# Low parts of the query weights by GpSimd, half of the second stream's choices during the query projection, and three split buffers in the dense expert sum

## The reference, cut to what matters

```
q = (h @ w_q).reshape(b, l, PEER_HEADS, 2, PEER_KEY_DIM // 2)
s = einsum('blhpk,hpnk->blhpn', q, sub_keys)
sv, si = top_k(s, 16)
cand = sv[..., 0, :, None] + sv[..., 1, None, :]
cv, ci = top_k(cand, 16)
expert = i1 * 128 + i2           # i1, i2: keys picked by ci
gate = softmax(cv)
act = gelu(einsum('tkd,td->tk', u[expert], h))
out = einsum('tk,tkd->td', gate * act, v[expert])
x = x + g2 * out; y = rmsnorm(x, final_g)
```

## Time and profile before

| | us |
|---|---|
| median of three timed runs | 3150.67 (3147.31 to 3153.22) |
| the profiled execution | 3154.65 |
| its span, first to last instruction | 3152.6 |
| busy: PE / DVE / ACT / POOL | 2352.2 / 2236.9 / 1229.7 / 1153.3 |
| query projection, from the first half of wq to the last copy of its result | 1713 to 1816 |
| u stretch, to the last `expert_act` | 1816 to 2511 |
| scatter of stream 1 | 2512 to 2592 |
| dense v, 128 iterations | 2593 to 3134 |
| last adds, norm, stores | 3134 to 3153 |

### The profile page before, as it was taken

How to read it: one execution, slowest core, us unless ns; L and a number is a source line. 1 busy time by engine, 2 the same in 40 slices (tenths; PEclk the granted TensorE clock), 3 DMA queues, 4 the chain that set the end, 5 groups by cost and what they waited for, 6 DMA issues and landing times.

```text
span 3152.6 us, 38773 instructions
## 1 busy us (share of the span) xinstructions
PE 2352.2 (75%) x15046; PEld 2063.5 (65%) x15046; DVE 2236.9 (71%) x2892; ACT 1229.7 (39%) x1951; POOL 1153.3 (37%) x773
## 2 busy tenths in 40 slices
PE   6899999999989998999998910000330079998997
PEld 2588889988877887999987910000330068786886
DVE  1344446878888753444545899999999889895885
ACT  1233334555455643433343300001990184342433
POOL 0000000255645510000000032787888647674660
PEclk8899999999999999999999955555555579997999
DMA  9888775545444478766553487999999869996993
GB/s 380 335 308 290 292 294 191 191 142 175 147 154 157 155 258 327 282 243 226 191 187 134 148 335 251 405 422 422 422 421 422 360 187 373 352 364 225 329 370 132
DMA packets 149033, 866.74 MB, mean 275 GB/s; under 512 B 17858, under 2 KB 30162, under 8 KB 70626
## 3 DMA queue, kind: packets, MB, share of 16 engines
q1 hardware_dynamic: 67698, 447.32, 38.7%
q0 software_dynamic: 70992, 406.08, 33.3%
q10 hardware_dynamic: 10160, 10.88, 1.0%
HBM read 836.81 MB, written 27.39 MB: 274 GB/s over the span
## 4 chain that ended last, share of the span: by engine, by line
PE 53%; DVE 14%; POOL 13%; DMA 8%; issue 8%; ACT 3%; DVEq 0%; SPq 0%; ACTq 0%; POOLq 0%
PE bank L1682 30%; POOL u_ring L673 13%; PE bank L2049 8%; PE bank L1668 7%; DMA raw<-in_tiles 3%; PE bank L1707 2%; DVE w_lo L1098 2%; DMA v_got<-in_v_rest,expert 2%; DVE u_ring L1561 2%; DMA u_ring<-in_peer_u,expert 2%; PE bank L2032 2%; DVE conv L1212 1%; DVE peer_g L1589 1%; DMA v_raw<-in_v_dense 1%; DVE y_w L1270 1%
## 5 line engine op out<-in xcount | busy, mean ns | idle before, releaser
L1098 DVE TENSOR_TENSOR w_lo<-raw,w_hi 128x1024 fp32r<-128x1024 f32 x482 | 638.6, 1339 | 573.8 <-ACT w_hi L716 568.9
L716 ACT ACTIVATE w_hi<-raw 128x1024 fp32r<-128x1024 f32 x482 | 501.1, 1058 | 654.0 <-PE bank L1682 347.9
L673 POOL DMA_INDIRECT u_ring<-in_peer_u,expert x256 | 479.9, 1875 | 411.4 <-PE bank L1682 212.9
L1682 PE MATMUL bank<-h_lo,w_hi 128*128 128x256 f32 x2048 | 594.0, 290 | 26.3 <-DVE w_lo L1098 17.3
L1561 DVE CUSTOM_DVE_ANT_0 u_ring<-u_ring,h_t 128x2048 f32<-128x2048 f32 x256 | 580.4, 2289 | 28.4 <-DMA u_ring<-in_peer_u,expert 26.7
L1682 PE MATMUL bank<-h_hi,w_lo 128*128 128x256 f32 x2048 | 583.0, 285 | 0.0
L1682 PE MATMUL bank<-h_hi,w_hi 128*128 128x256 f32 x2048 | 582.8, 285 | 0.0
L1682 PEld LDWEIGHTS bank<-h_lo,w_hi 128*128 128x128 f32 x2048 | 396.2, 193 | 69.2 <-issue 30.5
L680 POOL DMA_INDIRECT v_got<-in_v_rest,expert x256 | 342.5, 1338 | 229.1 <-DVE peer_g L1589 180.8
L1682 PEld LDWEIGHTS bank<-h_hi,w_lo 128*128 128x128 f32 x2048 | 396.7, 194 | 0.9
L1682 PEld LDWEIGHTS bank<-h_hi,w_hi 128*128 128x128 f32 x2048 | 396.1, 193 | 0.0
(11 more groups left out here) (304 smaller groups left out, 4568.9 us busy)
## 6 DMA issues: line engine op xcount, KB each, us to landing
raw<-in_tiles SPq DMA_DIRECT2D x337, 1024.0 KB, 5.4
v_raw<-in_v_dense SPq DMA_DIRECT2D x128, 660.0 KB, 6.9
s_t<-in_states POOLq DMA_DIRECT2D x8, 512.0 KB, 7.0
y_hi_rows<-y_hi_e POOLq DMA_DIRECT2D x16, 256.0 KB, 2.4
y_lo_rows<-y_lo_e POOLq DMA_DIRECT2D x16, 256.0 KB, 6.2
gate_rows<-gate_buf ACTq DMA_DIRECT2D x8, 512.0 KB, 4.6
y_hi<-y_hi_rows POOLq DMA_DIRECT2D x1, 4096.0 KB, 27.4
y_lo<-y_lo_rows POOLq DMA_DIRECT2D x1, 4096.0 KB, 17.0
```

The costliest lines, as they stand in the source:

```text
L673: pool.indirect_dma_start(u_ring[:, U_SLOT[e]], None, a["peer_u"][0], bass.IndirectOffsetOnAxis(ap=expert[:, s, k:k + 1], axis=0)).then_in ...
L716: act.activation(w_hi[:, i % RING], raw[:, slot % SLOTS, (n % 2) * 2 * CH:(n % 2 + 1) * 2 * CH], ACT.Copy) \
L1098: dve.tensor_tensor(w_lo[:, i % RING], raw[:, n // 2 % SLOTS, (n % 2) * 2 * CH:(n % 2 + 1) * 2 * CH], w_hi[:, i % RING].bitcast(F32), ALU. ...
L1682: ins = pe.matmul(spot if x.shape[1] == KT else spot.rearrange("p (s t) -> p s t", s=NS), w[:, col], moving, start=start and k == 0 and m ...
```

## The change

1. The low parts of the 32 halves of wq are made by POOL, with a semaphore of their own (`lo_wq`), in front of its gathers. DVE does none of them.
2. `choose(1, 0)` and `choose(1, 1)` run on DVE during the projection, right behind `choose(0, 0)` and `choose(0, 1)`. With no w_lo to place, DVE goes on in the list at one pause alone, counted over the chooses of a block (pause 9, 5, 1, 0 for j = 0, 1, 2, 3), where it copies the result of the next block (L1525). The semaphores of the choices are kept by stream, and `choose(1, 2)` and `choose(1, 3)` alone have an `expert_act` in their pauses.
3. Dense v has three split buffers instead of two, and three raw buffers instead of four. SP no longer waits for the scatter in front of raw tile 3.
4. The eight spreads of g2 lie behind every second iteration (64, 66, ... 78) instead of every one, and ACT's copies at 68, 70, ... 82. SP's loads of the rows of g2 and final_g move from i = 34 to 42, that of x3 from 98 to 106, with the same waits.

```
-TABLE = 4
+TABLE = 3
+DENSE = 3
@@ SP
-                        sp.wait_ge(lo_done, SPLIT_NO[last] + 1)
+                        if SPLIT_NO[last] < WQ_NO:
+                            sp.wait_ge(lo_done, SPLIT_NO[last] + 1)
+                        else:
+                            sp.wait_ge(lo_wq, SPLIT_NO[last] + 1 - WQ_NO)
...
-                if i == TABLE - 1:
-                    sp.wait_ge(scat_done, NS * BATCHES)
...
-                if i == 34:
+                if i == 42:
                     sp.wait_ge(dense_done, 32)
...
-                if i == 98:
+                if i == 106:
                     sp.wait_ge(dense_done, 96)
@@ POOL
+            for i in range(WQ_NO, len(SPLIT)):
+                n = SPLIT[i]
+                pool.wait_ge(hi_done, i + 1)
+                pool.wait_ge(split_used, SPLIT[i - RING] + 1)
+                pool.tensor_tensor(w_lo[:, i % RING], raw[:, n // 2 % SLOTS, (n % 2) * 2 * CH:(n % 2 + 1) * 2 * CH],
+                                   w_hi[:, i % RING].bitcast(F32), ALU.subtract).then_inc(lo_wq, 1)
@@ ACT
-                if i >= 2:
-                    act.wait_ge(dense_done, i - 1)
-                act.activation(v_hi[:, i % 2], v_raw[i % TABLE][:], ACT.Copy).then_inc(v_hi_done, 1)
+                if i >= DENSE:
+                    act.wait_ge(dense_done, i - DENSE + 1)
+                act.activation(v_hi[i % DENSE][:], v_raw[i % TABLE][:], ACT.Copy).then_inc(v_hi_done, 1)
...
-                if 68 <= i < 76:
-                    n = i - 68
+                if 68 <= i < 84 and i % 2 == 0:
+                    n = (i - 68) // 2
@@ DVE
-                if n not in SPLIT_NO:
+                if n not in SPLIT_NO or SPLIT_NO[n] >= WQ_NO:
                     return
...
+            def pause(j):
+                if pauses[0] == (9, 5, 1, 0)[j]:
+                    advance_to(min(FIRST["wq", j] + 2 * HALVES + LEAD, N_HALVES + LEAD))
+                pauses[0] += 1
 
             for j in range(4):
                 advance_to(min(FIRST["wq", j] + HALVES + LEAD + 3, N_HALVES + LEAD))
-                limit = min(FIRST["wq", j] + 2 * HALVES + LEAD, N_HALVES + LEAD)
-                choose(0, j, lambda: next_half(limit))
+                pauses[0] = 0
+                choose(0, j, lambda: pause(j))
+                if j < 2:
+                    choose(1, j, lambda: pause(j))
...
-            for j in range(4):
+            for j in range(2, 4):
                 choose(1, j, take)
@@ PE
-                if 64 <= i < 72:
-                    n = i - 64
+                if 64 <= i < 80 and i % 2 == 0:
+                    n = (i - 64) // 2
```

More of the change, by code:

```diff
@@ L312, in program @@
         coef_d = at("coef_d", [P, NS, N_KEYS, P], F32, 0)
[L314 to L318, removed]
+        v_raw = [at(f"v_raw{n}", [P, V_DENSE], F32, kib) for n, kib in enumerate((191, 196.15625, 145))]
+        v_hi = [at(f"v_hi{n}", [P, V_DENSE], F32R, kib) for n, kib in enumerate((152, 157.15625, 177))]
+        v_lo = [at(f"v_lo{n}", [P, V_DENSE], F32R, kib) for n, kib in enumerate((128, 133.15625, 171.84375))]
+        c_hi = [at(f"c_hi{n}", [P, NS, P], F32R, kib) for n, kib in enumerate((162.5, 163.5, 182.25))]
+        c_lo = [at(f"c_lo{n}", [P, NS, P], F32R, kib) for n, kib in enumerate((164.5, 165.5, 183.25))]
         v_got = [at(f"v_got{n}", [P, V_REST], F32, kib) for n, kib in
@@ L428, in program @@
         score_in = sem("score_in")
-        gate_max = sem("gate_max")
+        gate_max = [sem(f"gate_max{s}") for s in range(NS)]
         gate_exp = sem("gate_exp")
-        chosen = sem("chosen")
+        chosen = [sem(f"chosen{s}") for s in range(NS)]
         x2_saved = sem("x2_saved")
@@ L487, in _ @@
             sp.dma_start(x2_rows, x2_t[:]).then_inc(x2_saved, 16)
-            sp.wait_ge(chosen, 4 * NS)
+            for s in range(NS):
+                sp.wait_ge(chosen[s], 4)
             sp.wait_ge(split_used, N_HALVES)
@@ L1386, in choose @@
                                               in1=keyf[:, s, 1, mine], op0=ALU.mult, op1=ALU.add))
-                dve.tensor_copy(expert[:, s, mine], key_f[:]).then_inc(chosen, 1)
+                dve.tensor_copy(expert[:, s, mine], key_f[:]).then_inc(chosen[s], 1)
             def normalise(s):
@@ L1593, in dense_lo @@
                 dve.wait_ge(v_hi_done, i + 1)
-                if i >= 2:
-                    dve.wait_ge(dense_done, i - 1)
-                dve.tensor_tensor(v_lo[:, i % 2], v_raw[i % TABLE][:], v_hi[:, i % 2].bitcast(F32), ALU.subtract) \
+                if i >= DENSE:
+                    dve.wait_ge(dense_done, i - DENSE + 1)
+                dve.tensor_tensor(v_lo[i % DENSE][:], v_raw[i % TABLE][:], v_hi[i % DENSE][:].bitcast(F32), ALU.subtract) \
                     .then_inc(v_lo_done, 1)
@@ L1993, in _ @@
                 if n in SPLIT_NO:
-                    pe.wait_ge(lo_done, SPLIT_NO[n] + 1)
+                    if SPLIT_NO[n] < WQ_NO:
+                        pe.wait_ge(lo_done, SPLIT_NO[n] + 1)
+                    else:
+                        pe.wait_ge(lo_wq, SPLIT_NO[n] + 1 - WQ_NO)
                 work(n)
```

24 lines of the change are left out of this document (11 added, 13 removed).

## The result

The changed kernel takes 3112.17 us (median of four runs, 3107.02 to 3116.14) where the kernel before takes 3148.99 on the same chip (four runs): ratio 0.9887, 95% interval 0.9858 to 0.9916, 36.8 us less. A second comparison on another chip, with nine runs of before, gave 3108.27 against 3153.57, ratio 0.9856 [0.984, 0.9873]. The forecast was 3117, in a range from 3094 to 3138.

What follows compares the result with a forecast made beforehand. It took PE and DVE to bound the projection, DVE then DMA the u stretch, DVE dense v, except a stall at g2. Terms -38 - 1.3 + 3 + 2.7 = -33.6 from 3150.7 gave 3117 us, range 3094 to 3138.

Steps and rivals of the forecast that it cites:

- g2 every second iteration: Dense v, iterations 66 to 75: 41 us lost to stalls, 3 of PE's delay reaching DVE; gain 38 us, bounds 34 and 41.
- the 4.35 us: Dense v: the part of PE's 7.4 us delay from eight spreads that the third split buffer absorbs before DVE is held.
- the ring: At g2 in dense v: PE waits for ACT's copy, which ACT cannot reach before PE ends another iteration; 41.0 us lost.
- Start of dense v: v_hi(2) no longer waits for PE's iteration 0, so v_lo(2) starts at about 2597.8 instead of 2599.13: -1.3 us.
- Three raw buffers: Dense v: one raw buffer fewer leaves loads less time to land; cost +3 us, bounds -5 and +12.
- My slack of 8.4 us: Dense v: the time a raw load may take to land with three raw buffers, against 12.1 with four.
- rival C: Dense v: raw buffers starve the loop, 3170 us, marked by ACT's v_hi waiting over 50 us for v_raw; chance 0.05.
- Projection and u stretch: DVE's freed work moves the u stretch's end by -22.3 us, POOL's lock gives back 25: +3 us, bounds -22 and +26.
- c: What POOL's w_lo costs DVE in lock waits during the chooses: 25 us, bounds 0 and 48.
- The price of w_lo on POOL: Query projection: no row had w_lo on POOL; the nearest, L601, takes 2.41 us at least, 2.70 in the median.
- Rival B: Query projection: POOL's w_lo takes 2.7 us or more and short casts are locked too, 3137 us; chance 0.13.
- PE's stops behind the copies: Query projection: PE waits about 8 us at blocks 1 and 2 for DVE's late result copies; nobody waits for PE.

Runs made afterwards that it cites:

- projection part alone: Against the kernel before: only w_lo of wq moved to POOL and choose(1, 0), choose(1, 1) made early, dense v untouched; 3151.69 us, ratio 1.0009.
- spacing alone: Against the kernel before: only g2's spreads and copies moved to every second iteration, with two split and four raw buffers; 3120.19 us, ratio 0.9905.
- buffers alone: Against the kernel before: only dense v's three split and three raw buffers, no scatter wait, g2's spreads still at eight iterations in a row; 3110.82 us, 0.9881.
- two pieces: Against the changed kernel: each w_lo on POOL made by two 128x512 instructions instead of one 128x1024; run twice, 3104.24 and 3104.68 us.
- four pieces with a wait: Against the changed kernel: each w_lo on POOL in four 128x256 instructions, an already met semaphore wait ahead of each; 3123.3 us, ratio 0.9894.
- four-piece runs: Against the changed kernel: each w_lo on POOL in four 128x256 instructions, no added wait; run twice, 3120.65 and 3120.39 us.

## Why the prediction was right, point by point

**g2 every second iteration, -38.** Measured -40.7 between iterations 66 and 75, and PE falls behind as worked out: in the chain of waits after, a pair of iterations is 7.43 us of matmuls and one spread (1.12 in its record, 1.05 in the chain), 8.49 from pair to pair (8.4 predicted).

```profile
2852.78 7.43 PE bank L2067 x36
2861.25 7.43 PE bank L2067 x36
2869.73 7.44 PE bank L2067 x36
```

Part of the lag comes out behind iteration 75: the 37 iterations to 112 are 3.5 us longer. 40.7 - 3.5 is 37.2, beside the 38. How long the stall is varies by itself: with the dense part untouched (projection part alone) iterations 66 to 75 take 68.91 us instead of 74.75, and 75 to 112 take 150.26 instead of 147.18. Taken over 66 to 112, the two executions of the untouched dense part average 220.6 and the nine with both edits 184.3: 36.2 us, still close to the 38. The two ends that I gave are measured too: spacing alone, nothing absorbed, was put at 34 and gives 32 to 35; the 4.35 us for what a third split buffer absorbs is 5.5, from one execution. What the prediction had wrong is the attribution. It gave the 38 us to the spacing, and the run with the buffers alone reaches 35.6 without it (623.1 to 587.5): each of the two edits opens the ring, and the second adds about 5.

**Start of dense v, -1.3.** From L to v_lo of iteration 2 pass 89.1 us instead of 90.1: -1.0.

**Three raw buffers, +3: mis-sized.** The runs with three and four raw buffers give -3, within what executions differ by, and from v_lo of iteration 2 to that of 66 pass 245.5 to 251.4 us in the ten executions with three raw buffers and both of SP's waits moved, 248.8 to 252.0 in the three with four: no cost is seen, and 0 or a little less is what the runs allow. My slack of 8.4 us was not contradicted; the landings of 2595 to 2760 are 6.4 to 11.5 us with a median of 7.3 (before), and only the tail of them passes it. That tail is shorter with three raw buffers: in nine executions 4 to 11 landings of iterations 5 to 109 are over 8.4 us, where there were 18. But the step counted every stop of v_raw as one of DVE. The waits from 2590 to 3090 after the change:

```profile
ACT v_hi L1030 <- DMA v_raw<-in_v_dense: 211.9, 92, 9.6
ACT v_hi L1030 <- PE bank L2067: 71.2, 33, 4.1
DVE v_lo L1611 <- ACT v_hi L1030: 26.9, 19, 2.0
DVE peer_g L1604 <- DMA v_got<-in_v_rest,expert: 19.8, 23, 3.3
```

ACT waits 211.9 us for v_raw. I had written that over 50 would be rival C. As a marker that was wrong: with three split buffers ACT is free to run ahead of PE, so it stands at the load, where it used to stand at PE (291.1 us for PE and 15.8 for v_raw in the same stretch before). The run with three raw and two split buffers shows that it is the split buffer: there ACT waits 263.8 us for PE and 26.3 for v_raw, in the same stretch:

```profile
ACT v_hi L1020 <- PE bank L2049: 263.8, 118, 4.2
ACT v_hi L1020 <- DMA v_raw<-in_v_dense: 26.3, 8, 8.4
```

What counts is the third line of the change's waits, DVE's wait for v_hi, 26.9 us in the whole stretch against 55.5 before.

**Projection and u stretch, -22.3 + c with c = 25.** Without waits, six chooses of 15.6, three copies of 0.6 and the first 0.9 us of the seventh put T at F + 96.3. Measured are 118.5, 118.3 and 116.4, so c is 22.2, 22.0 and 20.1. Lock waits alone are 20.7 us in the first. L - F is 759.7 on average with the new order and 758.8 without (five executions): +0.9 where -22.3 + 25 gave +2.7. The gain of 22 us in DVE's work is there, and lost to the lock as foreseen. That c comes out at the end of the u stretch is shown by the versions of w_lo: from the second run of two pieces (c 16.1, L - F 755.3) to the four pieces with a wait (c 36.6, L - F 775.2) the stretch grows by 19.9 us for 20.5 of c. The size of c is in part luck. POOL was through with w_lo at 1814.6 and not at 1830, so three chooses stood beside it and not 3.6; the first of them took 26.0 us, the next two, less a copy each, about 21, where I had 22. Two details missed: `cand`, which I put among the waiting ones, found POOL at rest (0.71 us), and `hot` is at 1.3 to 1.4 on average, just below the 1.5 to 2.5 that I had named. The first take was at 1863.95 instead of 1872; of these 8 us, 4.8 are F's.

**The price of w_lo on POOL**, for which no row of before stood: 2.45 us on average, 2.41 in the median and 2.38 to 2.72 over all 32, so the lower end of L601's 2.41 to 2.70. Rival B needed the upper end and locked casts. Casts do wait for POOL, as the two pieces show, but no cast in front of T waited for a whole w_lo: the one slow `part_f` (0.43 us from 1825.75) ended with a gather of POOL, at 1826.17. The prediction said that no row shows such an instruction beside POOL. The trace of before had some, beside gathers: this `expert` takes 0.36 us instead of 0.18 and ends 0.01 behind the gather.

```profile
1823.20 0.94 POOL L673 DMA_INDIRECT u_ring<-in_peer_u,expert  x1 [0.30 <-issue]
1823.78 0.36 DVE L1387 CAST expert<-key_f 128x32 uint32<-128x32 f32 x1
```

**PE's stops behind the copies**, put at 8 us each at blocks 1 and 2: at block 1 it is 8.1 us; at block 2 there is none in the profiled execution of the result and 3.1 us in the second; behind the last half, at the last copy, PE stops for 12.6 us (6.4 in the second), until DVE reaches that copy: at 1834.13, where the prediction had about 1843. PE ends its last half at 1822 and not at 1834 to 1840. POOL's gather 6 waits for PE behind that last stop, until 1846.46 (1826.3 before), but DVE, which sets T, is never idle for more than 0.3 us between F and T, so none of it is paid.

**Sum.** -40.8 in the dense part (put at -36.3) and +0.9 in front of it (put at +2.7) are -39.9, where the forecast had -33.6; the two comparisons of medians give -36.8 and -45.3. The dense part is 4.5 us better than forecast and the part in front 1.8. Taken from the averages, as above, the 4.5 lie in front of iteration 66 (iterations 2 to 66: 248.7 on average instead of 251.4, where +3 was forecast) and not at g2. These 2.7 us are within what executions differ by, so the runs show that the +3 was not paid, and no more.

## What to carry to other kernels

Where a stretch loses time in a ring of waits through three engines, look for every edge of the ring that can be opened, and price them together: here two edits of the change open the same ring, each is worth 32 to 36 us of the dense part alone, and both together 41.

Before work is moved from VectorE to GpSimd, count the VectorE instructions that will run beside it and what each waits: here 20.5 us of work moved and 20.7 us of waits came back. Pieces of 1.3 us were better than pieces of 2.4, and gapless strings of pieces of 0.7 worse than both, by 8 and 13 us at the first take, because such a string left one VectorE instruction out until its end.

A limit for a wait, written down ahead of a change, belongs to the engine that paces the loop. A wait of an engine that has slack moves with the number of buffers: here ACT's for v_raw went from 26 us to over 200 with one more split buffer, and the kernel was no slower.

## What the runs showed of the hardware that I had not expected

A VectorE instruction that has begun and needs the shared turn can be passed over by many GpSimd instructions, 30 in the longest cases here: 21.55, 21.56, 21.56 and 13.30 us for an add of 0.69, each ending 0.55 us behind the last of a gapless string of 128x256 instructions. In the second strings of the four-piece runs, and ahead of the 13.30 us in the same string, VectorE instructions got their turn after one piece (a `hot` took 1.1 us). What decides between the two is open. A semaphore wait that is already met leaves no gap between two GpSimd instructions (0.70 us a piece with it and without).

One-input casts and `tensor_scalar` of 128x32 and 128x64 elements wait for GpSimd as two-input work does: 0.69, 0.41 and 0.36 us on average (`expert`, `part_f`, `part_i`) with GpSimd in halves, 0.18, 0.20 and 0.17 where it was at rest. Those that met a half took 1.19 to 1.32 us.
